# A joint stage of softmax attention and gated DeltaNet on one core: the order of its attention units, the size of an accumulator group, and the place of the sampled tile

## The reference, cut to what matters

```
# softmax attention of the prompt: 8 heads of 64, three branches per head
for each query tile, head:
    for branch in (compressed, selected, window):
        s = q @ k.T * scale                # compressed: 31 keys; the others: all keys up to the tile
        p = exp(s - max(s)) masked;  o[branch] = (p @ v) / sum(p)
    no = gate0 * o[0] + gate1 * o[1] + gate2 * o[2];   out = no * silu(g)
# gated DeltaNet, 4 heads, chunk by chunk, a state S handed from chunk to chunk
Tinv = inverse(I + strict_lower(...))      # by doubling levels
v_new = Tinv @ (v*beta - (k*beta*exp(G)) @ S)
o = (q*exp(G)) @ S + att @ v_new;   S = S*exp(G_last) + k_dec.T @ v_new
out = rmsnorm(o) * silu(g)
```

## Time and profile before

| | us |
|---|---|
| median of 3 runs (lowest to highest) | 2570.82 (2570.56 to 2584.24) |
| the profiled execution's own time | 2579.64 |
| its span, first to last instruction | 2577.7 |
| TensorE busy (share of the span) | 2209.9 (86%) |
| VectorE, ScalarE, GpSimd busy | 1268.7, 797.6, 303.2 |
| mean granted TensorE clock | 0.872 |
| the joint stage, first layer | 378 to 751 |

### The profile page before, as it was taken

One profiled execution on the slowest core, in us unless ns is written; L12 is line 12 of the kernel. 1 busy time (PEld: TensorE's weight loads), 2 busy tenths in 40 slices (PEclk: granted clock), 3 DMA queues, 4 the chain that ended last, 5 costly groups with the idle time before them and its releaser, 6 DMA issues. The chain is left out here.

```text
span 2577.7 us, 35901 instructions
## 1 busy us (share of the span) xinstructions
PE 2209.9 (86%) x12280; PEld 1635.0 (63%) x12280; DVE 1268.7 (49%) x2972; ACT 797.6 (31%) x1646; POOL 303.2 (12%) x516
## 2 busy tenths in 40 slices
PE   6989857788878999997889897687887799999977
PEld 3644456677757888886345444566776588888863
DVE  2253363655545666664223524545655356666532
ACT  2211112333334444440222211123334345444302
POOL 0000000000023433320000000000000333334100
PEclk9999866888869999995989897678988789999869
DMA  5443110000046887762044431000000758778430
GB/s 188 144 140 105 49 24 2 9 1 1 1 105 163 189 182 166 170 141 105 7 149 150 152 90 40 23 1 9 1 1 2 167 144 192 161 164 185 102 110 37
DMA packets 176170, 243.08 MB, mean 94 GB/s; under 512 B 50086, under 2 KB 132806, under 8 KB 175308
## 3 DMA queue, kind: packets, MB, share of 16 engines
q1 hardware_dynamic: 151404, 173.56, 25.1%
q0 software_dynamic: 24576, 67.14, 11.1%
HBM read 223.69 MB, written 25.50 MB: 97 GB/s over the span
## 5 line engine op out<-in xcount | busy, mean ns | idle before, releaser
L619 PE MATMUL bank<-W,hT 128*128 128x512 f32 (+3 forms) x1152 | 450.8, 543 | 34.0 <-DMA W<-in_w_in 21.1
L1045 POOL DMA_DIRECT2D SHARED<-in_cache_nsa_kv x256 | 152.3, 595 | 1988.8 <-issue 1581.6
L619 PEld LDWEIGHTS bank<-W,hT 128*128 128x128 f32 x1152 | 217.1, 195 | 225.6 <-issue 176.2
L988 PE MATMUL bank<-XT,W 128*128 128x256 f32 (+1 forms) x768 | 250.7, 462 | 0.0
L977 ACT ACTIVATE XT<-bank 128x512 f32<-128x512 f32 x256 | 140.0, 593 | 132.5 <-PE bank L970 132.4
L1045 POOL DMA_DIRECT2D PS<-in_cache_nsa_kv x256 | 150.7, 589 | 138.8 <-issue 126.0
L988 PEld LDWEIGHTS bank<-XT,W 128*128 128x128 f32 x768 | 134.9, 190 | 49.7 <-issue 36.9
L1421 DVE TENSOR_REDUCE mx<-bank 128x1 f32<-128x31 f32 (+4 forms) x192 | 74.8, 390 | 185.1 <-PE bank L1273 183.6
L970 PE MATMUL bank<-CF,RP 128*128 128x128 f32 x1024 | 146.7, 289 | 9.6 <-DVE RP L958 8.6
L1233 ACT ACTIVATE Pr<-bank,mx 128x31 f32<-128x31 f32 (+4 forms) x192 | 85.7, 447 | 204.2 <-DVE mx L1422 204.0
L372 DVE COPY UP<-bank 128x512 f32<-128x512 f32 (+3 forms) x36 | 21.6, 605 | 250.4 <-PE bank L619 250.3
(11 more groups left out here) (383 smaller groups left out, 3627.2 us busy)
## 6 DMA issues: line engine op xcount, KB each, us to landing
SHARED<-in_cache_nsa_kv SPq DMA_DIRECT2D x256, 128.0 KB, 5.6
SHARED<-in_cache_nsa_kv POOLq DMA_DIRECT2D x256, 128.0 KB, 5.3
PS<-in_cache_nsa_kv SPq DMA_DIRECT2D x256, 128.0 KB, 6.1
PS<-in_cache_nsa_kv POOLq DMA_DIRECT2D x256, 128.0 KB, 5.7
W<-in_w_in SPq DMA_DIRECT2D x48, 512.0 KB, 4.2
XS<-scratch_conv_p SPq DMA_DIRECT2D x24, 384.0 KB
PW<-in_state_nsa_win SPq DMA_DIRECT2D x16, 512.0 KB, 3.8
Wo<-in_w_out SPq DMA_DIRECT2D x4, 2048.0 KB, 11.9
```

Of the source, the lines that this page charges most:

```text
L619: return nc.tensor.matmul(bk((c * NTILE + t) % BANKS)[:, 0:b - a], hT[:, k, t * P:(t + 1) * P], W[:, k // 2, k % 2, 0:b - a], start=(k == ...
L988: mm = nc_(self.v).tensor.matmul(out, self.v['W1'][:, kv, s, :], seg[:, s], start=(s == 0), stop=(s == SEG // PAIRS - 1))
L1045: e.dma_start(where[side * HD:(side + 1) * HD, slot, :, :], A['cache_nsa_kv'][l, page].rearrange("(p r) a g d -> p r (a g d)", r=PAIRS)[:, ...
```

## The change

- Units go by query tile (3, 0, 1, 2), within it by head, and within a head by branch (1, 2, 0). Six units, two heads with three branches each, form a group in the accumulator bank (384 of its columns).
- At a group's end VectorE does the three small operations on 6 values a row in place of 8, one product of 384 columns into TB, and, after the next unit's maximum, one reduction over the branches and one product of 128 columns into the result. There are 16 groups a layer in place of 12.
- The tiles go (0, 4, 1, 2, 3). The sampled tile's `ready` steps stand between tile 0's levels, its states between tile 1's levels. Four steps are new for it: `masked` (QM), `added0` and `added1` (the two halves of the state update on VectorE), and `sums1` (TensorE's second half) in place of `state4`.
- A unit's cost in the planner is 256 plus the keys, the planner's share is 0.95 instead of 0.93, and two units stand ahead of the first step.

```
-    TILES = (4, 0, 1, 2, 3)
+    TILES = (0, 4, 1, 2, 3)
-    state = lambda t: [(f"state{i}", t) for i in range(5 if t == 4 else 4)]
-    beside = {4: [], 0: state(4) + ready(1), 1: state(0) + ready(2), 2: state(1) + ready(3), 3: state(2)}
-    DELTA = ready(4) + ready(0)
+    state = lambda t: [(f"state{i}", t) for i in range(4)]
+    sampled = [("masked", 4)] + state(4) + [("added0", 4), ("sums1", 4), ("added1", 4)]
+    beside = {0: ready(4), 4: state(0) + ready(1), 1: sampled + ready(2), 2: state(1) + ready(3), 3: state(2)}
+    DELTA = ready(0)
...
-    QTS, BRANCHES, DEEP, AHEAD = (3, 2, 1, 0), (1, 2, 0), 2, 0.93
-    units = [(qt, br, h) for qt in QTS for br in BRANCHES for h in range(NH)]
+    QTS, BRANCHES, DEEP, AHEAD = (3, 0, 1, 2), (1, 2, 0), 2, 0.95
+    units = [(qt, br, h) for qt in QTS for h in range(NH) for br in BRANCHES]
+    NU, GROUP = len(units), 6
-    cost = [P + keys(u) for u in range(NU)]
-    ORDER, spent, u = [], 0, 0
+    cost = [2 * P + keys(u) for u in range(NU)]
+    ORDER, spent, u = [("unit", 0), ("unit", 1)], cost[0] + cost[1], 2
...
-                if h == 0 and u:
-                    e.wait_ge(merged, u // NH)
+                if u and u % GROUP == 0:
+                    e.wait_ge(merged, u // GROUP)
+                o = (h % 2 * 3 + br) * HD
...
-                    mm = nc.tensor.matmul(bk(OUT)[:, h * HD:(h + 1) * HD], PT[0:m, u % 2, j, :], vv, start=(j == 0), stop=(j == -(-n // P) - 1))
+                    mm = nc.tensor.matmul(bk(OUT)[:, o:o + HD], PT[0:m, u % 2, j, :], vv, start=(j == 0), stop=(j == -(-n // P) - 1))
...
-                if t == 4 and what in ("state3", "state4"):
+                if t == 4 and what in ("state3", "sums1"):
...
-                    link(nc.vector.tensor_scalar(fac[:, :], SUM[:, br, :], 1e-30, None, ALU.max))
+                    link(nc.vector.tensor_scalar(fac[:, :, :], SUM[:, (u - 2) // GROUP % 2, :, :], 1e-30, None, ALU.max))
...
-                    nc.vector.tensor_tensor(hb(dst[:, :]), hb(bk(OUT)), b_(fac[:, :], 2, [P, NH, HD]), ALU.mult).then_inc(merged, 1)
+                    out = bk(OUT)[:, 0:GROUP * HD].rearrange("p (h b d) -> p h b d", h=2, b=3)
+                    nc.vector.tensor_tensor(TB[:, :, :, :], out, b_(fac[:, :, :], 3, [P, 2, 3, HD]), ALU.mult).then_inc(merged, 1)
...
-                    if br != FIRST:
-                        link(nc.vector.tensor_tensor(NO[:, :], NO[:, :], TB[:, :], ALU.add))
-                    if br == LAST:
-                        link(nc.vector.tensor_tensor(MIX[:, qt, 256:768], NO[:, :], U[qt][:, NG:NG + 512], ALU.mult))
+                    link(nc.vector.tensor_reduce(NO[:, :, :], TB[:, :, :, :].rearrange("p h b d -> p h d b"), AX.X, ALU.add))
+                    link(nc.vector.tensor_tensor(MIX[:, qt, 256 + first * HD:256 + (first + 2) * HD], NO[:, :, :].rearrange("p h d -> p (h d)"),
+                                                 U[qt][:, NG + first * HD:NG + (first + 2) * HD], ALU.mult))
...
+                if what == "masked":
+                    for i in range(4):
+                        dve.link(e, f"qm{i}", nc.vector.tensor_tensor(QM[i], b_(QKT[:, i, 0:64], 1, [P, NB, 64]), cf('own', 64), ALU.mult))
...
-                    if t == 4:
-                        sampled_states(0)
-                        values_by_row(1)
-                if what == "state4":
+                if what == "added0":
+                    sampled_states(0)
+                    values_by_row(1)
+                if what == "added1":
                     sampled_states(1)
```

More of the change, by code:

```diff
@@ L1082, in delta_attention @@
     DELTA += state(3)
-    QTS, BRANCHES, DEEP, AHEAD = (3, 2, 1, 0), (1, 2, 0), 2, 0.93
-    FIRST, LAST = BRANCHES[0], BRANCHES[-1]
-    units = [(qt, br, h) for qt in QTS for br in BRANCHES for h in range(NH)]
-    NU = len(units)
+    QTS, BRANCHES, DEEP, AHEAD = (3, 0, 1, 2), (1, 2, 0), 2, 0.95
+    units = [(qt, br, h) for qt in QTS for h in range(NH) for br in BRANCHES]
+    NU, GROUP = len(units), 6
     def keys(u):
@@ L1125, in delta_attention @@
     mx = sb(scope, "mx", [P, DEEP, 2])
[L1126 to L1129, removed]
+    SUM = sb(scope, "SUM", [P, 2, 2, 3])
+    fac = sb(scope, "fac", [P, 2, 3])
+    TB = sb(scope, "TB", [P, 2, 3, HD])
+    NO = sb(scope, "NO", [P, 2, HD])
     bk, cf, cb, ident, MIX = v['bk'], v['cf'], v['cb'], v['ident'], v['MIX']
@@ L1166, in delta_attention @@
         if what == "state0":
-            dn += ([f"qm{i}" for i in range(4)] if t == 4 else []) + [f"{n}{t}" for n in ("ks", "r")]
+            dn += [f"{n}{t}" for n in ("ks", "r")]
             pn += [f"ks{t}"]
@@ L1178, in delta_attention @@
             an += [f"rt{t}"]
-        if t == 4 and what in ("state3", "state4"):
-            q = int(what == "state4")
-            pn += [f"sv{q}"]
+        if what == "masked":
+            dn += [f"qm{i}" for i in range(4)]
+        if t == 4 and what in ("state3", "sums1"):
+            pn += [f"sv{int(what == 'sums1')}"]
+        if what in ("added0", "added1"):
+            q = int(what == "added1")
             dn += [f"ss{hp}{q}{j}" for hp in range(2) for j in "nms"] + ([] if q else ["vm1"])
@@ L1233, in unit @@
                     nc.scalar.activation(Pr[:, u % DEEP, 0:n], sbank(u)[:, 0:n], ACT.Exp, scale=SCALE, bias=mx[:, u % DEEP, 1:2],
-                                         accum_out=SUM[:, br, h:h + 1]).then_inc(exped, 1)
+                                         accum_out=SUM[:, u // GROUP % 2, h % 2, br:br + 1]).then_inc(exped, 1)
             for what, x in ORDER:
@@ L1386, in _ @@
                         pe.done(e, f"su{t}", mm)
-                if t == 4 and what in ("state3", "state4"):
+                if t == 4 and what in ("state3", "sums1"):
                     for hp in range(2):
                         mm = nc.tensor.matmul(bk(hp), kd[0:n, hp * P:(hp + 1) * P], VM[0:n, :, hp * P:(hp + 1) * P], start=True, stop=True)
-                    pe.done(e, f"sv{int(what == 'state4')}", mm)
+                    pe.done(e, f"sv{int(what == 'sums1')}", mm)
         @block.vector
@@ L1406, in unit @@
             def unit(u):
-                hb = lambda ap: ap.rearrange("p (h c) -> p h c", c=HD)
-                end = u >= 2 and units[u - 2][2] == NH - 1
+                end = u >= 2 and (u - 2) % GROUP == GROUP - 1
                 if end:
                     qt, br, h = units[u - 2]
-                    dst = NO if br == FIRST else TB
+                    first = h - 1
+                    gates = U[qt][:, NGATE:NGATE + 3 * NH].rearrange("p (b h) -> p h b", b=3)[:, first:first + 2, :]
                     e.wait_ge(exped, u - 1)
-                    link(nc.vector.tensor_scalar(fac[:, :], SUM[:, br, :], 1e-30, None, ALU.max))
-                    link(nc.vector.reciprocal(fac[:, :], fac[:, :]))
-                    link(nc.vector.tensor_tensor(fac[:, :], fac[:, :], U[qt][:, NGATE + br * NH:NGATE + (br + 1) * NH], ALU.mult))
+                    link(nc.vector.tensor_scalar(fac[:, :, :], SUM[:, (u - 2) // GROUP % 2, :, :], 1e-30, None, ALU.max))
+                    link(nc.vector.reciprocal(fac[:, :, :], fac[:, :, :]))
+                    link(nc.vector.tensor_tensor(fac[:, :, :], fac[:, :, :], gates, ALU.mult))
                     e.wait_ge(used, u - 1)
-                    nc.vector.tensor_tensor(hb(dst[:, :]), hb(bk(OUT)), b_(fac[:, :], 2, [P, NH, HD]), ALU.mult).then_inc(merged, 1)
+                    out = bk(OUT)[:, 0:GROUP * HD].rearrange("p (h b d) -> p h b d", h=2, b=3)
+                    nc.vector.tensor_tensor(TB[:, :, :, :], out, b_(fac[:, :, :], 3, [P, 2, 3, HD]), ALU.mult).then_inc(merged, 1)
                 if u < NU:
@@ L1505, in _ @@
                 if what == "state0":
-                    for i in range(4) if t == 4 else ():
-                        dve.link(e, f"qm{i}", nc.vector.tensor_tensor(QM[i], b_(QKT[:, i, 0:64], 1, [P, NB, 64]), cf('own', 64), ALU.mult))
                     pe.wait(e, f"ks{t}")
```

2 lines of the change are left out of this document (1 added, 1 removed).

## The result

The kernel after takes **2583.7 us** (median of 20 runs), the kernel before 2572.1 in the runs beside it: ratio **1.0042**, 95% interval 1.0025 to 1.0060, so 11 us slower where 20 faster were forecast. A ratio of 0.001 is 2.57 us, 1.3 us a layer; all that follows is counted so.

What follows compares the result with a forecast made beforehand. TensorE is busiest in the joint stage, but some stretches run at half clock. Terms -6 - 8 - 2 + 3 + 3 = -10 us a layer, -20 in all, take the median 2570.82 to 2551 us; range 2515 to 2605.

Steps and rivals of the forecast that it cites:

- The end: Joint stage's tail after the last step: 5 units left instead of 14, 17.2 us instead of 28.0; net -6 a layer.
- The runs: Eight 31-key units in a row at low clock beside the steps: interleaving branches removes them, -8 us a layer.
- the merges: VectorE's merging of groups, 16 instead of 12, with a strided reduction of 0.75 us: +3 us a layer.
- the rival that hangs the drops on `state3`: Clock drops follow the `state3` chains, which all stay, so interleaving gives nothing: -2 us a layer, 2567 us, chance 0.24.
- a sign of trouble: Sign of a wrong forecast: TensorE waiting for a group's product for more than 12 us a layer.
- The sampled tile: Its states moved beside query tile 0's short units: 24.3 us lost there against 21.4 before; +3 us a layer.
- the start: Joint stage's first stretch, 14.4 us idle before: two units ahead and tile 0's long matrices earlier, -2 us a layer.
- The slower one: Rival: the sampled stretch, units 24 to 47, at half clock, mean below about 0.75; +13 us a layer, 2597 us, chance 0.30.

Runs made afterwards that it cites:

- c: Kernel before with the new units (order, groups of six, two ahead of the steps, planner's cost and share) but the old chunk steps: ratio 0.9939.
- n: Kernel after with the planner's share `AHEAD` at 0.93 in place of 0.95: ratio 0.9921.
- o: Kernel after with the planner's share `AHEAD` at 0.97 in place of 0.95: ratio 1.0044.
- b: Kernel before with only the order of the chunk steps changed to the new one, units as before: ratio 0.9982.
- j: New units with old steps (as c), the sampled tile's state steps taken out of the list: ratio 0.9850.
- k: Kernel after with the sampled tile's state steps taken out of the list, all else in place: ratio 0.9906.
- e: Kernel after with the VectorE operations of the state updates cut from 512 to 8 columns: ratio 1.0031.
- f: Kernel after with the VectorE blocks `masked`, `added0` and `added1` each cut into two steps: ratio 0.9999.
- i: New units with old steps (as c), the planner's share `AHEAD` at 0.98 in place of 0.95: ratio 0.9925.

## Why the prediction was wrong

**The end** had the right length: from the last `n33` to the stage's end 18.5 us, 17.2 forecast. **The runs, the end and the merges together** stood at -11 a layer and run c, which has just these, the two leading units and the planner's new cost and share, measured -7.8. Among query tiles 1 and 2 the first profile of after has no low stretch of 16 us, the second has one of 17 us (623 to 640, clock 0.50), which begins with tile 1's `state3`: the rival that hangs the drops on `state3` is not quite out.

**The merges.** The reduction took 0.583 us, not 0.75; TensorE's wait came to 12.7 us where 12.2 was forecast, past the 12 that I had named as a sign of trouble. The size was right, its meaning not: the wait has no price per merge, it hangs on where each stands: 2.9 us (n) to 16.3 (o) for the same 16 merges. At unit 37 I saw the merge behind `added0` and priced it 2.2; it took 4.76.

**The sampled tile, +3, and the start, -2, are the steps that failed.** Together they put the move of the steps at +1 us a layer. Beside the new units it measured +13 (c to after, some 5 either way by the intervals), beside the old ones -2 (b, some 3 either way). The working of the +3 gave the new place 24.3 us lost and took off the 21.4 that the stretch from 428 to 482 us lost before, as if such a loss belonged to the chain and came and left with it. Runs j and k show that most of it stays when the chain is taken out: up to unit 24, j loses 47 and 43 us in its two layers against 53 in c; in units 24 to 47, k loses 29 against the 34 to 37 of after. By the ratios the states cost 6 us a layer more in the new place than in the old, twice the +3, but the intervals allow 0 to 12. The other 7 (3 to 11) are there without the states, and by the profiles they lie mainly in the start: k, where as in after tile 0's ready chain comes first, loses 53 us up to unit 24, j 47 and 43. In n, with the same order of steps as after, the start loses 46: this too moves with the deal.

**The terms were added as if the deal did not matter.** Each term was priced at the place of a unit among the steps, and these places hang on the second digit of `AHEAD`. The sum, -20 us, is what b and c give when added and what run n measures, but that n meets it is in part luck: its tail is 24.0 us where 17.2 was forecast, its units 24 to 47 lose 31 where 24.3 was priced, and of the three deals the two others lose 11 us. No rival said this. The slower one had the right stretch and sign, 2597 for 2584 measured, but not the mechanism: its half clock did not come (0.77 and, in the second profile, 0.71 there, about its threshold of 0.75). The rule on the swinging clock in "TensorE: Matmul & The Clock Gate" of the Trainium skill, section "A second HAM failure mode: psum-queue depth-cycling", agrees with the trace of after in direction: units 24 to 47, with 20.3 of 80.4 us idle, have a clock of 0.77, the two rows behind them, with 13.2 of 78.8 and 12.5 of 67.0 idle, 0.87 and 0.95. Between runs it orders nothing: a quarter less idle time, in e, did not lift the clock of that stretch, and in k it idles only 13.0 of 64.3 us and runs at 0.68.

**Open.** That one deal gains 20 us and its neighbour loses 11 is shown as idle time of TensorE, 68 against 77 to 79 us a layer. Which wait sets it stays open: between after and n the wait for the accumulator falls by 10 us and that for the exponentials grows by 4, and over the other runs neither goes with the time. The idle time as a whole does: in the six runs with all matmuls at ratios of 0.989 to 0.996 TensorE idles 65 to 69 us a layer, in those from 0.998 up 73 to 86, all but f (0.9999, 68 to 70).

## What to carry to other kernels

A list that interleaves two chains by hand is one draw among many: deal it again with the planner's constants a few per cent to either side before crediting or blaming an edit, since here that moved the time by 30 us, more than any part of the change. Take the halves of a change apart and add them up; what is missing is their interaction. Time lost in a stretch belongs to the stretch until a run without the suspect has shown otherwise; here most of it stayed, in the old place and in the new.

## Not expected of the hardware

The states of the sampled tile, with 13 us of TensorE work a layer, cost 11 at the stage's start. Run e took 5.5 us of TensorE's idle time out of a stretch, and the granted clock there stayed at 0.77 and 0.72, the layers no shorter than 369.0 and 372.2 us. And what repeats with a list is TensorE's idle time, not the length: both layers of i idle 68 us (68.2 and 68.0), but one lasts 359.8 us at a clock of 0.80 and the other 351.9 at 0.83, while both layers of c last 358.4 and 358.5.
